# Input transposes of an expert pair, moved between the gate/up matmuls of the pair before

## The reference, cut to what matters

```
hid = (jax.nn.silu(jnp.einsum("nd,edf->nef", x, P["moe_w_gate"][l]))
       * jnp.einsum("nd,edf->nef", x, P["moe_w_up"][l]))
routed = jnp.einsum("nef,efd->nd", hid * gates[:, :, None], P["moe_w_down"][l])
```

## Time and profile before

| | |
|---|---|
| time, median of 3 runs | 1886.65 us (1884.95 to 1886.7) |
| the profiled execution | 1884.84 us, of which the span of the profile is 1883.3 us |
| PE busy | 1735.3 us, 92% of the span |
| DVE, ACT, POOL busy | 24%, 18%, 6% |
| granted PE clock, mean | 0.959 of full speed |
| routed experts, layer 1 and 2 | 442 to 936 us and 1361 to 1853 us of the span |

### The profile page before, as it was taken

The page is one execution under the profiler, slowest core; times in us unless marked ns, Lnnn a source line. Parts: engine busy times, 40 slices in busy tenths (PEclk is TensorE's granted clock), DMA queues, the critical chain, the costliest instruction groups (busy, mean ns, idle before and its releaser), DMA issues.

```text
span 1883.3 us, 24716 instructions
## 1 busy us (share of the span) xinstructions
PE 1735.3 (92%) x8887; PEld 1089.0 (58%) x8887; DVE 451.2 (24%) x1196; ACT 338.2 (18%) x780; POOL 108.4 (6%) x143
## 2 busy tenths in 40 slices
PE   3999999868999999999979999995799999999995
PEld 2778777754444444544558878784644444444443
DVE  2015444242111111111131344334311111111112
ACT  0110340121111111111120113302011111111111
POOL 3000000001000000001010000000000000000000
PEclk9999998978999999999989999897799999999997
DMA  9975222325999999999988532241399999999990
GB/s 372 382 282 180 90 90 96 134 84 216 419 420 418 419 420 420 419 419 414 415 326 347 221 121 90 73 159 57 114 379 420 420 419 420 419 419 419 418 399 34
DMA packets 86179, 554.78 MB, mean 295 GB/s; under 512 B 15612, under 2 KB 15792, under 8 KB 21552
## 3 DMA queue, kind: packets, MB, share of 16 engines
q1 hardware_dynamic: 72576, 528.51, 69.3%
q0 software_dynamic: 13488, 24.71, 3.8%
HBM read 570.69 MB, written 4.75 MB: 306 GB/s over the span
## 4 chain that ended last, share of the span: by engine, by line
PE 89%; DVE 5%; DMA 3%; issue 1%; ACT 1%; POOL 0%; DVEq 0%; SPq 0%; ACTq 0%; POOLq 0%
PE PS L906 23%; PE PS L557 13%; PE PS L929 12%; PE PS L950 11%; PE PS L451 6%; PE PS L789 4%; PE PS L836 3%; PE PS L509 3%; PE PS L486 2%; PE PS L572 2%; PE PS L619 1%; PE PS L864 1%; DMA ring<-in_expert_blocks 1%; PE PS L775 1%; DMA region<-in_c 1%
## 5 line engine op out<-in xcount | busy, mean ns | idle before, releaser
L906 PE MATMUL PS<-ring,region 128*64 128x512 f32 x2048 | 462.7, 598 | 1.8 <-ACT region L1147 1.7
L906 PEld LDWEIGHTS PS<-ring,region 128*64 128x64 f32 x2048 | 155.7, 138 | 297.4 <-issue 291.2
L557 PE MATMUL PS<-region,ring 128*128 128x256 f32 x1088 | 245.2, 381 | 0.0
L950 PE MATMUL PS<-region 128*128 128x256 f32 x1024 | 242.3, 380 | 0.0
L929 PE MATMUL PS<-ring,region 128*64 128x512 f32 x1024 | 233.8, 598 | 0.2
L557 PEld LDWEIGHTS PS<-region,ring 128*128 128x128 f32 x1088 | 203.8, 190 | 33.5 <-issue 6.3
L950 PEld LDWEIGHTS PS<-region 128*128 128x128 f32 x1024 | 184.7, 190 | 23.1 <-issue 3.2
L1547 DVE SCALAR_TENSOR_TENSOR region<-region,PS 128x256 f32<-128x256 f32 x64 | 26.9, 421 | 696.9 <-ACT region L1154 696.9
L451 PE MATMUL PS<-const,region 128*128 128x128 f32 (+1 forms) x877 | 138.0, 290 | 42.1 <-DMA region<-in_c 18.9
L451 PEld LDWEIGHTS PS<-const,region 128*128 128x128 f32 (+1 forms) x877 | 107.2, 148 | 110.4 <-issue 72.7
L929 PEld LDWEIGHTS PS<-ring,region 128*64 128x64 f32 x1024 | 67.8, 136 | 130.8 <-issue 130.2
(11 more groups left out here) (235 smaller groups left out, 1113.9 us busy)
## 6 DMA issues: line engine op xcount, KB each, us to landing
ring<-in_expert_blocks SPq DMA_DIRECT2D x384, 1024.0 KB, 17.6
ring<-in_blocks SPq DMA_DIRECT2D x120, 1024.0 KB, 10.9
h_table<-region POOLq DMA_DIRECT2D x4, 544.0 KB, 3.6
region<-in_w_kvk POOLq DMA_DIRECT2D x2, 640.0 KB, 16.9
region<-in_mla_w_ukv POOLq DMA_DIRECT2D x2, 512.0 KB, 20.7
region<-h_table,region POOLq DMA_INDIRECT x64, 8.4
const<-in_consts POOLq DMA_DIRECT2D x1, 640.0 KB, 8.6
region<-in_x_prompt POOLq DMA_DIRECT2D x1, 512.0 KB, 11.8
```

The lines of the kernel that those rows point to most:

```text
L557: last = pe.matmul(PS[:, j % 2, m * T:(m + 1) * T], w[:, k, m * P:(m + 1) * P], hT[:, k, :], start=(k == 0), stop=(k == KC - 1))
L906: last = pe.matmul(PS[e * CAP:(e + 1) * CAP, 0, :], xe[:, k, e * CAP:(e + 1) * CAP], w[:, k % 4, :], start=(k == 0), stop=(k == KC - 1), s ...
L950: last = pe.matmul(PS[:, 4 + c // 2, (c % 2) * T:(c % 2 + 1) * T], og[:, c * P:(c + 1) * P], hot, start=False, stop=True, skip_group_check ...
```

## The change

`xe` gets a second buffer, and pairs use them in turn. `transpose_inputs` goes. In its place `transpose_input(g + 1, c)` issues one transpose, and `gate_up(g)` calls it behind its steps: chunks 0, 1, 2 and 3 behind steps 0, 1, 2 and 3, chunks 4 and 5 behind step 5, chunks 6 and 7 behind step 6. `combine` is divided into six and two chunks instead of four and four, and its first matmul always releases two slots. In pair 0, which has no combine beside it, the first hidden transpose releases them. On ACT the input copies of g+1 go ahead of the tanh of g.

```diff
-        xe = view(12480, KC, P)
+        xe = [view(12480, KC, P), view(17408, KC, P)]
...
+                    def transpose_input(g, c):
+
+                        if c == 0:
+                            pe.wait_ge(xg_in[g % XG], pe_gathers[g % XG] + 16 * (g // XG + 1))
+                        if c % 4 == 0 and (g >= 1 or c):
+
+                            pe.wait_ge(xe_ready, done + (2 * g + c // 4))
+                        last = transpose(PS[:, 1, (c % 4) * P:(c % 4 + 1) * P], xg[:, g % XG, c * P:(c + 1) * P])
+                        if c % 4 == 3:
+                            last.then_inc(xe_tr, 1)
+
+                    BETWEEN = ((0,), (1,), (2,), (3,), (), (4, 5), (6, 7), ())
...
+                            if k < KC - 1 and g + 1 < PAIRS:
+                                for c in BETWEEN[k]:
+                                    transpose_input(g + 1, c)
                         last.then_inc(gu_done, 1)
 
                     def transpose_hidden(g):
                         pe.wait_ge(hid_ready, done + (2 * g + 2))
                         for f in range(2):
                             last = transpose(PS[:, 0, f * P:(f + 1) * P], hid_rows[:, f * P:(f + 1) * P])
+                            if f == 0 and g == 0:
+                                release(last, 2)
                         last.then_inc(hid_tr, 1)
...
+                    def combine(g, part):
+
+                        if part == 0:
                             pe.wait_ge(hot_ready, pairs + (g + 1))
-                        for c in range(4 * half, 4 * half + 4):
+                        for c in (range(6), range(6, KC))[part]:
+                            if c % 4 == 0:
+                                pe.wait_ge(og_ready, done + (2 * g + c // 4 + 1))
                             last = pe.matmul(PS[:, 4 + c // 2, (c % 2) * T:(c % 2 + 1) * T], og[:, c * P:(c + 1) * P], hot,
                                              start=False, stop=True, skip_group_check=True)
-                            if c == 0 and frees:
-                                release(last, frees)
+                            if c == 0:
+                                release(last, 2)
                         last.then_inc(comb_done, 1)
...
                     for g in range(PAIRS):
-                        more = g + 1 < PAIRS
                         gate_up(g)
-                        if more:
-                            transpose_inputs(g + 1, 0, frees=2)
                         if g >= 1:
-                            combine(g - 1, 0, frees=0 if more else 2)
+                            combine(g - 1, 0)
                         transpose_hidden(g)
-                        if more:
-                            transpose_inputs(g + 1, 1)
                         if g >= 1:
                             combine(g - 1, 1)
                         down(g)
...
                     for g in range(PAIRS):
-                        half_tanh(g)
                         if g + 1 < PAIRS:
                             for half in range(2):
                                 take_inputs(g + 1, half)
+                        half_tanh(g)
                         for half in range(2):
                             take_out(g, half)
```

More of the change, by code:

```diff
@@ L905, in gate_up @@
                                 w = ring[:, n % RING_SLOTS, :].rearrange("p (k c) -> p k c", k=4)
-                                last = pe.matmul(PS[e * CAP:(e + 1) * CAP, 0, :], xe[:, k, e * CAP:(e + 1) * CAP], w[:, k % 4, :],
+                                last = pe.matmul(PS[e * CAP:(e + 1) * CAP, 0, :], xe[g % 2][:, k, e * CAP:(e + 1) * CAP], w[:, k % 4, :],
                                                  start=(k == 0), stop=(k == KC - 1), skip_group_check=True)
@@ L961, in _ @@
                     last.then_inc(list_tr, 1)
-                    for half in range(2):
-                        transpose_inputs(0, half)
+                    for c in range(KC):
+                        transpose_input(0, c)
                     for g in range(PAIRS):
-                        more = g + 1 < PAIRS
                         gate_up(g)
-                        if more:
-                            transpose_inputs(g + 1, 0, frees=2)
                         if g >= 1:
-                            combine(g - 1, 0, frees=0 if more else 2)
+                            combine(g - 1, 0)
                         transpose_hidden(g)
-                        if more:
-                            transpose_inputs(g + 1, 1)
                         if g >= 1:
@@ L976, in _ @@
                         down(g)
-                    for half in range(2):
-                        combine(PAIRS - 1, half, frees=0 if half else 2)
+                    for part in range(2):
+                        combine(PAIRS - 1, part)
                 pe.reg_add(passes, passes, npass)
@@ L1146, in take_inputs @@
                         act.wait_ge(xe_tr, done + (2 * g + half + 1))
-                        act.activation(xe[:, 4 * half:4 * half + 4, :].rearrange("p k s -> p (k s)"), bank(1), ACT.Copy).then_inc(xe_ready, 1)
+                        act.activation(xe[g % 2][:, 4 * half:4 * half + 4, :].rearrange("p k s -> p (k s)"), bank(1), ACT.Copy).then_inc(xe_ready, 1)
                     def half_tanh(g):
```

## The result

| | before | after |
|---|---|---|
| time, median of 4 runs each | 1885.8 us | 1994.04 us (1993.77 to 1995.06) |
| ratio | | 1.0575, 95% interval 1.0557 to 1.0593 |
| span of the profiled execution | 1883.3 us | 1992.2 us |
| PE busy | 1735.3 us | 1842.7 us |
| steady pair of experts | 15.15 us | 17.00 us |

The forecast was 1991 us in a range of 1970 to 2012. The change costs 108 us, 5.75%, and the span grows by 108.9.

The account below looks back on a forecast made before the run. PE bounds at 15.15 us a pair, weight loads at 15.6 close behind. Pairs 1 to 30 add 109.2 us, pair 0 5.3, pair 31 -0.5, DMA waits -7.8: +106.2 on 1884.84 gives 1991 us, range 1970 to 2012.

Parts of the forecast that it names:

- the DMA waits: Late in each layer's expert stage PE waits for weights; 7.8 us over two layers, expected to go with the change.
- the lead of the ring: Weight loads' head start in the expert stage: PE sets the pace (15.15 us a pair) until it is used up, then DMA.
- part 1: Input transposes at six places inside gate_up: each pays 0.15 us in and 0.145 out, 0.295 a place, 1.77 a pair.
- The rival with the weight load hidden: At the places in gate_up only the emptying is paid: 1.08 us a pair, 1948 us; chance 0.07 including a mixture.
- the dearer one: Places in gate_up cost 2.07 us a pair, or the hidden-row copy is late, or both: 2003 to 2030; chance 0.08.
- part 2: Behind gate_up, now combine: the change of shape stays, 0.15 becomes 0.20, +0.05 us a pair; the one into down stays.
- part 3: Combine 6 + 2: same eight matmuls, 2.79 us ahead of the hidden transposes keeps tanh and DVE covered; no gain or loss.
- parts 4 to 6: ACT's input copies ahead of tanh, gather wanted at step 0, slot releases: no new waits; the 7.8 us of DMA waits go.
- part 7: Ends of the expert stage: pair 0 pays 2.65 us a layer, 5.3 in all; pair 31 gives back 0.25, 0.5 in all.

Follow-up runs that it names:

- the light loads: The kernel before with the loads of the down weights cut to a quarter of their width; 1877.19 us, 0.9967 of before.

## Why the prediction was right

**The bound.** Right: PE at 15.15 us a pair, the loads at 15.6 behind it. A PE made 0.86 us a pair faster gained 3 to 6 us; one made 1.85 slower paid all of it less the DMA waits (60 x 1.85 - 7.35 = 103.65 over pairs 1 to 30, 103.9 measured). One side figure was off: 374 GB/s were forecast from 419 x 15.15 / 16.97, and 379 to 382 were measured. The loads need 15.6 us a pair at 419 GB/s, and the kernel before kept up 15.15 for most of the stage by using up the lead of the ring; 419 x 15.6 / 17.0 = 384 is the sum that fits.

**The price of a place (part 1).** Right, and slightly small: 0.295 us forecast from the two sides of one row of operations, 0.15 in and 0.15 out measured at lone transposes, 0.30 by the runs with two, three and six places. A steady pair is 17.00 us instead of 16.97; over 60 pairs that is the 2.0 us by which pairs 1 to 30 came out dearer (103.9 measured, 109.2 - 7.35 forecast). The rival with the weight load hidden (1948) is out: it needs 0.18 us a place, and a place costs 0.30. So is the dearer one: nothing waits for DVE's copy or on the semaphores inside `gate_up`.

**`gate_up` to combine, and combine 6 + 2 (parts 2 and 3).** 2.79 us forecast and measured; `down` 3.58 in both. The run with the places undone has part 3 without the rest, and it costs nothing; part 2 isn't in that run.

**ACT, gather, releases (parts 4 to 6).** No wait of PE for any of them in a steady pair. That the DMA waits go was right, with 7.8 us forecast and 5.9 (4.0 to 8.5, by the interval) measured by the light loads.

**Pair 0 (part 7).** The term that was mis-sized: 5.3 us forecast for two layers, 8.4 measured. The forecast took the clock for given. In the changed kernel `down` of pair 0 takes 5.05 us instead of the 3.65 of the earlier trace rows, and the stretches show the clock behind that (the number ahead of the DMA share is the granted clock). `down` of pair 0 in layer 1 and in layer 2, then the stretches in layer 1:

```profile
453.25 5.05 PE PS L947 x16
...
1428.05 5.35 PE PS L947 x16
```

```profile
450.00:453.00 3.00, 0.67 (x4) 0.20 (x2) 1.61 (x4) 0.38 (x1) 0.00 (x0) 0.95 0.98 415
453.00:455.00 2.00, 1.75 (x4) 0.53 (x6) 0.55 (x2) 0.00 (x0) 0.99 (x1) 0.50 0.73 217
```

The transposes that used to stand in front of PE's wait for DVE are now inside `gate_up`, PE has nothing to do from 450.3 to 452.3, and the clock goes from full to half. The two pieces together are 3.1 us longer than before, the whole of the difference.

The `gate_up` of pair 0 came out at 5.2 us more in both layers together, against the 5.3 forecast, and that agreement is luck. It is 1.96 us more in layer 1 and 3.28 in layer 2, for 2.65 forecast in each: `gate_up` starts at about half the clock, before and after. In the changed kernel the clock then rose earlier in layer 1 (0.55 in the first 4 us of `gate_up` and 1.00 in the next 4, where the kernel before had 0.50 and 0.89) and later in layer 2 (0.50 and 0.72, where the kernel before had 0.50 and 0.92).

That the idle time lowers the clock ahead of `down` is borne out by the other kernels, though no run changed it alone. In the five kernels with the transposes inside `gate_up` PE stands idle for 2.06 us ahead of the hidden transposes of pair 0, and in nine of these ten cases (two layers each) the clock is at 0.50 to 0.71 in the first 2 us of `down`; the tenth stays at 1.00 (layer 2 of the kernel with halved transposes). In the seven kernels with the transposes behind `gate_up` it idles for 1.39 to 1.48 us, and in all fourteen cases the clock stays at 1.00.

The three differences (2.0, 3.1 and -2.4 us in the part of the kernel that nothing touches) make 106.2 into 108.9.

No version here beats the kernel before with its work whole. The runs say why it is hard from PE's side: at 420 GB/s the loads leave a few us at most.

## What to carry to other kernels

Count the changes of the array's shape, not the operations: full-array transposes between matmuls that run side by side on halves cost 0.30 us for each place where they are put in, whether one, two or four stand there, so they belong in one block, beside work that already has that shape. Doing them in the halved shape (0.11 us more a chunk) beat six places, but not two, and not none. This change only moved work on the engine that sets the pace, so it had little to gain and much to lose; before such a change is made, find the second limit behind the first (here the loads, 0.45 us a pair away), since it tells what even a perfect outcome could be worth. And when work is taken out to test a bound, look at what was hidden under it: here 0.43 us taken from the wrong half uncovered another engine's chain.

## What was not expected of the hardware

The DMA busy share tells little about how much room is left: it was 0.97 in the changed kernel and 1.01 in the kernel with two places, where PE waited for no weights, and 1.01 to 1.02 in the kernel before and in those with less PE work, where the loads were the limit in the end. The time from issue to landing tells them apart: 7.2 and 8.9 us against 17.6 to 23.0 (medians of the pages). And the granted clock fell from full to half after 2.06 us in which PE had nothing to do, in nine cases of ten, where idling for 1.39 to 1.48 us left it at 1.00 in all fourteen.
